# A two-layer hybrid decoder step on one core: index queries for tokens 64 to 263 alone, and compression products set between the products of a mixing projection

## The reference, cut to what matters

```python
# (B), for one block of 128 queries; n_top = min(256, lk // 4), which is 64 for the prompt
dots = jnp.einsum('bthd,bsd->bths', iqb, ik) * IDX_DIM ** -0.5
score = jnp.einsum('bth,bths->bts', iwb, jax.nn.relu(dots))
score = jnp.where(kpos[None, None, :] <= qp[None, :, None], score, NEG)
sel = lax.top_k(score, n_top)[1]
s = jnp.where((sel <= qp[None, :, None])[:, :, None, None, :], s, NEG)   # s: scores against the picked keys
# (C), the compressed keys and values: 15 overlapping blocks of 32 tokens in the prompt
return jax.nn.silu(blk @ w1 + b1) @ w2
```

## Time and profile before

| | us |
|---|---|
| median of 3 runs | 980.28 |
| lowest, highest | 976.34, 982.62 |
| span of the profiled execution, first to last instruction | 979.2 |
| PE busy in it | 943.2 |
| DVE, ACT, POOL busy | 484.9, 304.5, 132.5 |

### The profile page before, as it was taken

How to read it: one execution, slowest core, us unless ns; L and a number is a source line. 1 busy time by engine, 2 the same in 40 slices (tenths; PEclk the granted TensorE clock), 3 DMA queues, 4 the chain that set the end, 5 groups by cost and what they waited for, 6 DMA issues and landing times.

```text
span 979.2 us, 17076 instructions
## 1 busy us (share of the span) xinstructions
PE 943.2 (96%) x6248; PEld 760.6 (78%) x6248; DVE 484.9 (50%) x1374; ACT 304.5 (31%) x659; POOL 132.5 (14%) x258
## 2 busy tenths in 40 slices
PE   9999999899999998999999999998999999899998
PEld 7888778777777776888888886787676867678887
DVE  4224548778643674134240345697785546731331
ACT  2135432247633113310121363331576311223000
POOL 0510000002032360000060000000020413600000
PEclk9999999999999999999999999999999999999999
DMA  7644417434199696334453435263342988952432
GB/s 266 203 157 162 165 54 332 178 140 173 44 332 386 215 385 225 135 129 139 163 182 139 146 135 200 108 286 129 146 162 86 373 306 310 378 173 89 162 140 87
DMA packets 56501, 188.98 MB, mean 193 GB/s; under 512 B 9186, under 2 KB 22882, under 8 KB 43874
## 3 DMA queue, kind: packets, MB, share of 16 engines
q1 hardware_dynamic: 43138, 138.56, 40.3%
q0 software_dynamic: 12992, 49.16, 13.2%
q10 hardware_dynamic: 288, 0.18, 0.1%
HBM read 177.47 MB, written 18.77 MB: 200 GB/s over the span
## 4 chain that ended last, share of the span: by engine, by line
PE 85%; DMA 5%; DVE 4%; ACT 3%; issue 1%; DVEq 1%; ACTq 1%
PE ps L868 22%; PE ps L998 17%; PE ps L1344 9%; DMA slab<-in_weights_dram 5%; PE ps L1237 5%; PE ps L1357 3%; PE ps L1351 3%; PE ps L880 3%; PE ps L893 2%; PE ps L1315 2%; PE ps L1148 2%; PE ps L1136 2%; PE ps L857 1%; PE ps L1216 1%; PE ps L1116 1%
## 5 line engine op out<-in xcount | busy, mean ns | idle before, releaser
L868 PE MATMUL ps<-hT,slab 128*128 128x264 f32 (+1 forms) x1184 | 274.9, 391 | 6.8 <-DMA slab<-in_weights_dram 5.9
L868 PEld LDWEIGHTS ps<-hT,slab 128*128 128x128 f32 (+1 forms) x1184 | 224.7, 192 | 47.2 <-DMA slab<-in_weights_dram 6.2
L998 PE MATMUL ps<-hT,slab 128*128 128x264 f32 x768 | 186.1, 400 | 1.7 <-DVEq L2109 1.7
L998 PEld LDWEIGHTS ps<-hT,slab 128*128 128x128 f32 x768 | 147.7, 196 | 34.5 <-DVEq L2037 3.2
L1369 ACT ACTIVATE arena<-ps 128x512 f32<-128x512 f32 (+21 forms) x152 | 69.8, 484 | 187.9 <-PE ps L868 66.7
L1344 PE MATMUL ps<-Y,slab 128*128 128x264 f32 x384 | 85.8, 386 | 0.0
L1344 PEld LDWEIGHTS ps<-Y,slab 128*128 128x128 f32 x384 | 73.0, 190 | 12.5
L1237 PEld LDWEIGHTS ps<-arena,w 128*128 128x128 f32 x512 | 58.4, 192 | 10.0 <-issue 6.6
L1763 DVE SCALAR_TENSOR_TENSOR arena<-arena,small 128x264 f32<-128x264 f32 x26 | 11.0, 488 | 110.1 <-ACT arena L1444 110.1
L1237 PE MATMUL ps<-arena,w 128*128 128x128 f32 x512 | 61.4, 278 | 0.0
L593 POOL DMA_DIRECT2D arena<-in_pages_kv_dram x64 | 33.3, 520 | 160.8 <-DVEq L2273 123.9
(11 more groups left out here) (365 smaller groups left out, 1208.8 us busy)
## 6 DMA issues: line engine op xcount, KB each, us to landing
slab<-in_weights_dram SPq DMA_DIRECT2D x86, 1024.0 KB, 5.0
arena<-in_pages_kv_dram SPq DMA_DIRECT2D x64, 256.0 KB, 8.3
arena<-in_pages_kv_dram POOLq DMA_DIRECT2D x64, 256.0 KB, 6.7
arena<-in_pages_kv_dram POOLq DMA_DIRECT2D x64, 128.0 KB, 7.8
arena<-in_pages_kv_dram SPq DMA_DIRECT2D x64, 128.0 KB, 10.3
out_dram<-in_state_win_dram POOLq DMA_DIRECT2D x2, 4088.0 KB, 29.4
arena<-in_state_hgrn_dram SPq DMA_DIRECT2D x2, 2048.0 KB, 27.9
out_dram<-arena POOLq DMA_DIRECT2D x2, 2048.0 KB, 7.3
```

The lines of the kernel that those rows point to most:

```text
L868: last = mm(ps[0:job[3], n % 2, 0:LT], v[:, k, job[2]:job[2] + job[3]], hT[:, k, :], start=(k == 0), stop=(k == KD - 1))
L998: last = mm(ps[:, bank, 0:LT], v[:, k, (d % 2) * 128:(d % 2) * 128 + 128], hT[:, k, :], start=(k == 0), stop=(k == KD - 1))
```

## The change

Three edits in the indexer and one in the compression. The index queries are projected, scaled and turned for tokens 64 to 263 (`ranked`, 200 columns) and no longer for 0 to 63. The scores of the first key block are formed, weighted and ranked for queries 64 to 127 (`late`, the upper 64 partitions) alone; the relu becomes two activations, and the mask of tokens 0 to 63 is copied from the causal mask. In the compression the eight products of `mix(2)` come first in each round of a loop, with two of the 16 w1 products behind each; the mark "h" now comes with the last of them.

```diff
+        ranked, late = slice(TOPK_P, LT), slice(TOPK_P, 128)
...
-                                last = mm(ps[:, n, 0:LT], stationary(name, job, k), XG[:, k, :], start=(k == 0), stop=(k == KD - 1))
+                                last = mm(ps[:, n, ranked], stationary(name, job, k), XG[:, k, ranked], start=(k == 0), stop=(k == KD - 1))
...
-                            last = mm(ps[:, n, 0:LT], stationary("iq0", job, k), XG[:, k, :], start=(k == 0), stop=(k == KD - 1))
+                            last = mm(ps[:, n, ranked], stationary("iq0", job, k), XG[:, k, ranked], start=(k == 0), stop=(k == KD - 1))
...
-                    mm(ps[:, bank, 0:128], Z[r, Z_IQ + j, 0:128], Z[r, Z_IK, 0:128], start=True, stop=True)
+                    mm(ps[late, bank, 0:128], Z[r, Z_IQ + j, late], Z[r, Z_IK, 0:128], start=True, stop=True)
...
-                for kv in range(2):
-                    for t in range(ST):
+                n = next(mixes)
+                v = arrived(f"m{n // KD}{n % KD // 2}")
+                for k in range(KD):
+                    turn = mm(ps[:, 2, 0:LT], v[:, k, (n % 2) * 128:(n % 2) * 128 + 128], hT[:, k, :], start=(k == 0), stop=(k == KD - 1))
+                    for i in (2 * k, 2 * k + 1):
+                        kv, t = i // ST, i % ST
                         last = mm(ps[:, kv, 0:36], w1[:, kv, t, :], XP[:, kv, t, :], start=(t == 0), stop=(t == ST - 1))
                 last.then_inc(cp_p.sem, cp_p.mark("h"))
-                mix(2)
+                turn.then_inc(mx_p.sem, mx_p.mark(f"m {n}"))
...
-                    A(RL[:, n % 2, :], ps[:, 4 + n % 2, 0:384], ACT.Relu).then_inc(pidx_a.sem, pidx_a.mark(f"relu {n}"))
+                    A(RL[late, n % 2, 0:128], ps[late, 4 + n % 2, 0:128], ACT.Relu)
+                    A(RL[:, n % 2, 128:384], ps[:, 4 + n % 2, 128:384], ACT.Relu).then_inc(pidx_a.sem, pidx_a.mark(f"relu {n}"))
...
-                    TT(Z[:, SLAB_OF[name][2][j][1], :], ps[:, n, 0:LT], rstd, ALU.mult).then_inc(iq_v.sem, iq_v.mark(f"q {n}"))
+                    TT(Z[:, SLAB_OF[name][2][j][1], ranked], ps[:, n, ranked], rstd[:, ranked], ALU.mult).then_inc(iq_v.sem, iq_v.mark(f"q {n}"))
...
-                top_keys(slice(0, 128))
-                top_keys(slice(128, 384))
-                TS(msk, acc, taken, NEG, ALU.not_equal, ALU.mult)
-                ve.drain()
-                TT(msk, msk, causal, ALU.add)
+                top_keys(late, slice(0, 128))
+                top_keys(slice(0, 128), slice(128, 384))
+                TC(msk[0:TOPK_P, 0:128], causal[0:TOPK_P, 0:128])
+                for r, c in ((late, slice(0, 128)), (slice(0, 128), slice(128, 384))):
+                    TS(msk[r, c], acc[r, c], taken, NEG, ALU.not_equal, ALU.mult)
+                ve.drain()
+                for r, c in ((late, slice(0, 128)), (slice(0, 128), slice(128, 384))):
+                    TT(msk[r, c], msk[r, c], causal[r, c], ALU.add)
```

More of the change, by code:

```diff
@@ L1764, in _ @@
                         ve.drain()
-                    nc.vector.stream_shuffle(T2[:, 0:n, :], x, ROTATED)
-                    TT(T1[:, 0:n, :], x, cosb(n), ALU.mult)
+                    w = ranked if name == "iq" else slice(0, LT)
+                    x, turned, kept = x[:, :, w], T2[:, 0:n, w], T1[:, 0:n, w]
+                    nc.vector.stream_shuffle(turned, x, ROTATED)
+                    TT(kept, x, cosb(n)[:, :, w], ALU.mult)
                     ve.drain()
-                    TT(T2[:, 0:n, :], T2[:, 0:n, :], sinb(n), ALU.mult)
+                    TT(turned, turned, sinb(n)[:, :, w], ALU.mult)
                     ve.drain()
-                    TT(x, T1[:, 0:n, :], T2[:, 0:n, :], ALU.add).then_inc(grp_v.sem, grp_v.mark(f"zr {name}"))
+                    TT(x, kept, turned, ALU.add).then_inc(grp_v.sem, grp_v.mark(f"zr {name}"))
                 ve.wait_ge(rows_a.sem, rows_a(l, "rows"))
@@ L1804, in _, with top_keys @@
                     ve.wait_ge(pidx_a.sem, pidx_a(l, f"relu {n}"))
-                    for t, c in enumerate((slice(0, 128), slice(128, 384))):
-                        STT(acc[:, c], RL[:, n % 2, c], iwP[:, t, h:h + 1], causal[:, c] if n == 0 else acc[:, c], ALU.mult, ALU.add)
+                    for t, (r, c) in enumerate(((late, slice(0, 128)), (slice(0, 128), slice(128, 384)))):
+                        STT(acc[r, c], RL[r, n % 2, c], iwP[r, t, h:h + 1], causal[r, c] if n == 0 else acc[r, c], ALU.mult, ALU.add)
                     ve.drain().then_inc(pidx_v.sem, pidx_v.mark(f"acc {n}"))
-                def top_keys(c):
+                def top_keys(r, c):
                     for _ in range(TOPK_P // 8):
-                        nc.vector.max(top8[:, :], acc[:, c])
+                        nc.vector.max(top8[r, :], acc[r, c])
                         ve.drain()
-                        nc.vector.match_replace(acc[:, c], top8[:, :], acc[:, c], taken)
+                        nc.vector.match_replace(acc[r, c], top8[r, :], acc[r, c], taken)
                         ve.drain()
```

## The result

| | median, us | lowest to highest | profiled span, us | mean granted clock |
|---|---|---|---|---|
| before (same chip) | 980.6 | 976.34 to 982.62 | 979.2 | 0.988 |
| after | 997.5 | 995.88 to 998.62 | 995.4 | 0.979 |

What follows compares the result with a forecast made beforehand. PE, busy 96% of the span, was taken as the bound. Span 979.2 - 6.9 (projections) + 0.8 (relus) + 6.4 (compression) = 979.5 us, so a median of 980.6; 8-in-10 range 974.5 to 985, chance of the same 0.94.

Steps and rivals of the forecast that it cites:

- part 2: Indexer scores and ranking: a small loss from the split relus, +0.4 us a layer, +0.8 in all, ends 0 and 2.
- The halved weight load of `dots`: Indexer's narrowed first product: its smaller weight load was taken to bring nothing, as it stands beside other matmuls.
- D: Query projections: the rival that 200 columns run no faster than 264, all but 0.1 us missing, 987.4 us; chance 0.04.
- Part 1: Query projections: 264 to 200 columns saves 3.45 us a layer, 6.9 in all, ends 0.1 and 7.2; hT in time.
- The same margin: Layer 0's query projections: the same order and 1.3 us to spare before PE would wait for hT, as in layer 1.
- Part 2's relus: Indexer: one relu split in two, 0.2 us at each of two places, +0.8 in all, ends 0 and 2.
- The mask: Ranking mask: three more DVE instructions cost 0; without cover some 0.5 us a layer, still beside a projection on PE.
- Part 3: Compression: PE idles 3.25 us behind alternating products, +1.5 us, and the clock falls in `mix(3)`, +1.7; 6.4 in all.
- The fall that I counted as saved: Compression: the half clock in `mix(2)` behind the 36-column products, costing 1.75 us, was expected to vanish with alternation.
- A: Compression: the rival that the clock doesn't fall behind the new idle stretch, `mix(3)` stays at 3.76 us, 977.2; chance 0.12.
- C: Compression: the rival that the clock falls inside the alternating stretch too, 1.7 us more a layer, 984.0; chance 0.13.
- B: Compression: the rival that narrow products' weight loads hide behind wide ones, 2.7 us off each layer, 975.2; chance 0.15.

Runs made afterwards that it cites:

- covered run: Changed kernel with wide first indexer product, one relu a head, alternating compression and one more mixing projection before the wait for hidden units; 0.9908 of before, 972.01 us.

## Why the prediction was wrong

**Where it failed** is one sentence of part 2: "The halved weight load of `dots` is worth nothing I can see: it stands beside other matmuls." I weighed the load that the narrowed product has less of, and took for granted that it would still stand beside other matmuls. By the edit it no longer can: the tile next to it has another shape. The term was put at 0, without bounds, and measured +8.9 us (eight pairs at 1.11), with +2.8 in `hi0` behind it. By the ratios, the run without the narrowed product gives 10.6 us back, the run with it alone costs 9.2, and the two runs that keep the narrow tile and take changes of shape away give 11.0 (all) and 8.7 (half) back. The changes of tile shape are the main cause, shown from both sides. The profile before could have put the question: in all eight pairs the tiles are 64*128 throughout, and where the shape does change, from L933's 8*128 tile to L941's, the load starts with its product (both at 111.92) and not ahead of it, as L942's does (112.13 and 112.24). What a change costs was in no row, so the step needed ends and not a zero. None of my rivals had it in mind either; D, the dearest, ended at 987.4.

**Part 1** was right in its mechanism: a pair of products at 200 columns takes 5.41 us in layer 1, as forecast, and hT is never waited for. Layer 1 gained the 3.4 us; layer 0 gained 2.1 in the changed kernel's profile, where its second pair of queries waits for a slab until 14.45 us; in the other runs with narrowed projections it gained 2.8 to 2.9, and 2.2 in the one with half the changes, again behind that slab. That is 5.5 to 6.3 us of the 6.9. "The same margin" in layer 0 left that slab out.

**Part 2's relus** were too small, within their bounds: 1.9 us (0.8 forecast, ends 0 and 2) where the products are quick, at the two places that I named. In the changed kernel the slow products cover them: PE waits 0.74 us for the last relu (127.45 to 128.19) where it waited 0.95. **The mask** cost nothing that shows: after is 5.25 us behind at the end of the gate projections (185.73 and 190.98) and 5.26 at the start of the compression (275.92 and 281.18).

**Part 3** was right step by step: alternating stretch 7.26 us (7.25), clock 1.00 in it, idle 3.36 us (3.25) with ACT as the releaser, `mix(3)` at 5.44 us (5.44), sum +3.5 a layer (+3.2). The covered run shows that the cover was the point. In the five kernels that alternate the clock stands at 1.00 through the stretch in all ten layers. The fall that I counted as saved is less sure: in the four kernels with the products in a row it came behind them in six of eight layers (`mix(2)` 4.90 to 5.33 us) and not in two (3.64), so one part of the sum came out right because both layers of the profiled execution of before had it. Rivals A (no clock fall behind the idle time) and C (a fall inside the alternating stretch) did not come true in either layer. B would need a shorter stretch: at 7.26 us, where one hidden load in each group gives 7.25, no second one was hidden. The pull-ahead of weight loads that I quoted for B from the Trainium skill ("TensorE: Matmul & The Clock Gate", Part 2) reached no further than one load here. D is out by 5.41 us.

**What stays open:** the mix behind the selection's wait. In the four kernels with the alternation and the idle time behind it, it fell to the half clock in all eight layers (5.29 to 5.51 us); with the covered alternation in two of two; with the products in a row in two of eight. PE's wait right ahead of it is 1.5 us before and after the change alike. So it seems to hang on what ran earlier, but no run here says on what. The gate projections' +2.4 us are a fall of the clock behind the same wait for a slab that cost more than before's; it is not there in the three runs with narrowed projections and wide products (5.5 us in both layers) or in the one with 64 columns throughout (3.83 and 5.30), and it is there in layer 1 alone of the run with half the changes (5.51 and 6.47). So it goes with the changes of shape, but I made no run that shows how.

## What to carry to other kernels

Before narrowing a matmul, look at the tile field of the matmuls next to it: if the narrow one has another weight tile shape than its neighbours, each change between them costs (0.28 us here between 64x64 and 64x128, 0.16 between 128x64 and 128x128), the overlap between row halves ends, and the clock may fall on top. Make all of them narrow, group them by shape, or leave them wide. And when two stretches of PE work are interleaved, ask what the second one covered: put other independent work in its place before the wait, or the idle time, and the clock behind it, cost more than was saved.

## What I had not expected of the hardware

- A stretch in which 64x64 and 64x128 tiles take turns was granted 0.50 (1.2 GHz) although PE never waits for another engine: 92 instructions in 40 us, where equal tiles had 126 in 10 us at 1.00.
- Narrow tiles by themselves are not slow: 283 instructions of 64x64 tiles in 15 us, 53 ns each.
- The price depends on the tiles: 128 rows with 64 and 128 columns in turn cost 0.16 us a change and left the clock at 1.00.
